# First experts' row lists by matrix products, and the slot table written in two passes of the expert loop

## The chip, the cores and the metric

One core of one Trainium2 chip runs the whole program as a single launch. The metric is the device time of that launch in microseconds. Before the change it is 1580.52 us, the median of three runs (1579.43 to 1581.09).

## What is computed

A residual block over 512 tokens and 16 meta tokens, width 1024: an input projection, a convolution branch and an mLSTM branch, an output projection, and then the part that this change touches, a mixture of 32 experts of which each token takes its best four.

```python
logits = xt @ router_w + router_b
top_val, top_idx = lax.top_k(logits, TOP_K)          # 4 of 32
gates = jax.nn.softmax(top_val, axis=-1)
...
hcat = xb @ w1[e] + b1[e]                            # 1024 x 2048
act = h_glu * sigmoid(1.702 * h_glu) * (h_lin + 1)   # both clamped at 7
ys = act @ w2[e] + b2[e]                             # 1024 x 1024
...
out = rms_norm(h + sum of gates * ys of each token's four experts)
```

## The kernel before, in words

The first third of the program (up to about 530 us) is the projections and the two branches. Then the router scores are made, and the expert loop runs: for expert 0 to 31 one pass, each with up to 96 tokens ("slots"). A pass multiplies the expert's tokens, transposed in `xT`, by the first weight matrix (192 records of L1613), DVE and ACT make the activation (L2096 to L2109), and a second product (192 records of L1642) makes the results, which DVE copies to `y_out` in three strips with the bias (L2127). The weights come through a ring of 12 buffers of 1 MB, one whole expert; SP asks for the next expert's piece as soon as TensorE has released a buffer (`ring_used`). A pass therefore needs two things: its weights, and its tokens.

The tokens come by row gathers that POOL issues one pass ahead. For pass n+1 POOL copies that expert's list into `piece_now` (L712) and issues three indirect DMAs from the row store `u_rows` into `xs` (L706, each after a small paced step, L705, that waits for a ring buffer). DVE transposes `xs` into `xT` (L2118) when all three have landed. Before POOL may gather, it must have sent the results of the pass before: three indirect DMAs of `y_out` into `y_rows` by `row_now` (L779, each after a step on `carrier`, L697), and it waits for their landing. So in steady state POOL does, in every pass: copy `row_now` (L769), three results out, wait for landing, copy `piece_now`, three gathers.

The lists come from a table in HBM, `slot_table`. For each of the 16 columns of token choices (4 tiles of 128 tokens times 4 choices) one indirect DMA of 128 four-byte entries writes the token's code to the place (slot, expert) (L730, `places_out`). After all 16 have landed, 16 loads bring the table back as `code_of` (L749), and 15 POOL operations (L755 to L759) turn it into `piece_of` (which rows to gather) and `row_of` (where results go) for all experts.

Two experts don't wait for the table. Expert 0's tokens are picked by TensorE directly: DVE makes a 0/1 matrix `in_slot` of tokens by slots (L1997), and TensorE multiplies the token rows by it (L1556); DVE transposes the product into `xT` (L2039). Expert 1's gather list is a product too: `in_second`, a 0/1 matrix for expert 1, times the token numbers (L1601), scaled by DVE into `piece_now` (L2048, 12 small operations). From expert 2 on, and for all result rows (expert 0's too), the table is needed.

The order on POOL around the change is written out by hand: eight scatters of the table as soon as the first two tiles' places are known, the three gathers for expert 1, eight more scatters paced by `ring_used` and `hid_mm` during pass 0, then the 16 loads, the arithmetic, a load of `last_g`, and the loop over the passes.

Of the kernel before, what the change touches and what calls it, by code (L numbers as in the profile page):

```python
# [78 lines left out]
PASSES = -(-SEQ // SLOTS)  # L79
SPREAD = 8  # L80
TURNS = 32 // SPREAD
NONE = 1 << 14
# [28 lines left out]
def hybrid_block(nc, x, meta_tokens, norm_mix_g, w_in, b_in, conv_dw_w, conv_dw_b, conv_ln_g, conv_ln_b,  # L111
# [3 lines left out]
    with ctx:  # L115
        def sem(name):
            return ctx.enter_context(nc.semaphore(name))
# [157 lines left out]
        in_second = at("in_second", [P, TT, SLOTS], F32, ffn_at[0] + size([P, (TT + 1) * SLOTS]) + size([P, P], BF16))  # L275
        token_no = at("token_no", [P, TT], F32, ffn_at[0] + size([P, (2 * TT + 1) * SLOTS]) + size([P, P], BF16))
        assert size([P, (2 * TT + 1) * SLOTS]) + size([P, P], BF16) + size([P, TT]) <= size([P, TG, 2 * GRP])
        hid = in_stage("hid", [P, TG, 2 * GRP])
# [90 lines left out]
        u2_mm, u2T_made, logits_mm, place_mm = sem("u2_mm"), sem("u2T_made"), sem("logits_mm"), sem("place_mm")  # L369
        moe_consts, mask_made, dest_made, table_set, table_written = sem("moe_consts"), sem("mask_made"), sem("dest_made"), sem("table_set"), sem("table_written")  # L370
        tables_made, passes_made, shifted, gate_exp = sem("tables_made"), sem("passes_made"), sem("shifted"), sem("gate_exp")
# [207 lines left out]
        def _(pool):  # L579
# [93 lines left out]
            nc.gpsimd.iota(code, [[TOPK * P, TT], [1, TOPK]], base=0, channel_multiplier=TOPK)  # L673
            nc.gpsimd.iota(token_no, [[P, TT]], base=0, channel_multiplier=1, allow_small_or_imprecise_dtypes=True)
# [3 lines left out]
            nc.gpsimd.iota(slot_no, [[32, TG], [1, SPREAD], [SPREAD, TURNS]], base=0, channel_multiplier=0, allow_small_or_imprecise_dtypes=True)  # L678
            chain(nc.gpsimd.memset(earlier, 1.0))
# [19 lines left out]
            def request_rows(turn=None):  # L699
# [10 lines left out]
            def gather(n, copied, turn=None):  # L710
# [3 lines left out]
                request_rows(turn)  # L714

# [3 lines left out]

            def places_out(i):  # L720

                pool.wait_ge(dest_made, i + 1)
                for m in range(TOPK * i, TOPK * (i + 1)):
                    if i >= 2:
                        late = m - 2 * TOPK
                        if late < KT - LATE:
                            pool.wait_ge(ring_used[late], 1)
                        else:
                            pool.wait_ge(hid_mm, late - (KT - LATE) + 1)
                    pool.indirect_dma_start(out=table, out_offset=bass.IndirectOffsetOnAxis(ap=dest[:, m:m + 1], axis=0),  # L730
                                            in_=code[:, m:m + 1], in_offset=None).then_inc(table_written, 16)
# [8 lines left out]
            pool.sem_inc(idx_step, 1)  # L740
# [5 lines left out]
            by_turn = table.rearrange("(x b a e) o -> b a x (e o)", b=TURNS, a=SPREAD, e=NE)  # L746
# [3 lines left out]
            pool.wait_ge(rows_in, 16 * CG * TURNS)  # L750
            for t in range(TG):
# [8 lines left out]
            pool.dma_start(last_g, final_norm_g.rearrange("(a d) -> a d", a=1).to_broadcast([P, D])).then_inc(last_g_in, 16)  # L760
            pool.wait_ge(y_emptied, 16 * KT)
            pool.wait_ge(passes_made, 1)
            passes = pool.value_load(n_passes[0:1, 0:1], min_val=1, max_val=PASSES)
            with pool.Fori(0, passes) as q:
# [7 lines left out]
                with pool.Fori(0, NE - 1) as e:  # L772
                    n = rows_of_expert(e)
                    pool.wait_ge(idx_step, n * IDX + 3 + TG)
                    for t in range(TG):

                        pool.wait_ge(y_made, n * TG + (t + 2))
                        carry_wait(1 + t)
                        pool.indirect_dma_start(out=y_dram, out_offset=bass.IndirectOffsetOnAxis(ap=row_now[:, t:t + 1], axis=0),  # L779
                                                in_=y_out[:, t], in_offset=None, bounds_check=last_row,  # L780
                                                oob_is_err=False).then_inc(y_stored, 16)

                    pool.wait_ge(y_stored, (q * (NE - 1) + e + 1) * (16 * TG))
                    carry_wait(1 + TG)
                    pool.wait_ge(xT_made, (n + 2) * TG)
                    gather(n + 2, n * IDX + 8 + TG, n + 2)

                n = rows_of_expert(NE - 1)
# [355 lines left out]
        def _(pe):  # L1144
# [455 lines left out]
            for i in range(TT):  # L1600
                last = nc.tensor.matmul(banks[0:SLOTS, SECOND_BANK, 0:1], in_second[:, i], token_no[:, i:i + 1], start=i == 0, stop=i == TT - 1)  # L1601
            last.then_inc(place_mm, 1)

            pe.wait_ge(passes_made, 1)
# [88 lines left out]
        def _(dve):  # L1693
            steps = [0]

            def chain(ins):

                steps[0] += 1
                ins.then_inc(dve_step, 1)
                dve.wait_ge(dve_step, steps[0])  # L1700
# [343 lines left out]

            dve.wait_ge(place_mm, TT + 2)
            for g in range(CG):
                for t in range(TG):
                    nc.vector.tensor_scalar(piece_now[32 * g:32 * (g + 1), t:t + 1], banks[32 * t:32 * (t + 1), SECOND_BANK, 0:1],  # L2048
                                            float(CG), float(g), ALU.mult, ALU.add).then_inc(tables_made, 1)
            dve.wait_ge(gate_exp, 1)  # L2050
# [174 lines left out]
```

## Time and profile before

| | |
|---|---|
| median of 3 runs | 1580.52 us |
| the profiled execution's own time | 1593.28 us |
| its span (first to last instruction) | 1591.5 us |
| mean granted TensorE clock | 0.987 of full |
| TensorE busy | 1537.9 us (97%) |
| DVE, POOL, ACT busy | 744.5, 533.4, 282.6 us |
| mean HBM and DMA traffic | 309 GB/s |

Times in the views are microseconds from the start of the span. "Idle before, releaser" says how long an engine did nothing before an instruction, and what ended it. The chain of waits follows the work that ended last back from the end; an entry "DMA a<-b" in it is the time from the issue of a transfer to its landing, and "issue" time in which nothing that the profile shows was waited for. TensorE's records are modelled at their ends, so back-to-back records mean that TensorE was fed, not that it was at its peak. The profiled execution is 12.8 us longer than the median of the runs.

### The profile page before, as it was taken

Reading aid. Unit: us, or ns where it says so; the run is one execution under the profiler, and the core shown is the slowest. Engines: PE = TensorE matmul, PEld = TensorE weight load, DVE = VectorE, ACT = ScalarE, POOL = GpSimd, SP = SyncE. Lnnn points to the kernel's source line nnn. Section 1 sums busy time; section 2 is a strip of 40 time slices with the busy share of each in tenths; the row PEclk is TensorE's granted clock in tenths of the full one; section 3 lists DMA queues with packets and bytes.
Section 4 is the critical chain, followed back from the end, with each engine's and each line's share of the span. In section 5 each row is a group of like instructions: output and inputs, shape, how many; then the busy total and the mean of one; then the engine's idle time right before and its main releaser. Section 6 shows DMA issues by size and latency. Waiting matters only on the chain.

```text
span 1591.5 us, 38141 instructions
## 1 busy us (share of the span) xinstructions
PE 1537.9 (97%) x15984; PEld 857.2 (54%) x15984; DVE 744.5 (47%) x1563; ACT 282.6 (18%) x406; POOL 533.4 (34%) x689
## 2 busy tenths in 40 slices
PE   7999999999999796999999999999999999999996
PEld 6998988877889532334333333433333343333334
DVE  4799898015242633344335334433533443353367
ACT  5333134346221300001001000100100010010001
POOL 7334333462343445222221222222122222212225
PEclk9999999999999898999999999999999999999998
DMA  7553243221276298999999999999999999999996
GB/s 218 159 181 111 78 144 98 84 75 53 80 291 229 67 334 348 362 417 420 419 418 418 420 418 418 420 418 418 418 419 418 416 421 419 418 419 420 418 418 248
DMA packets 132020, 492.27 MB, mean 309 GB/s; under 512 B 16301, under 2 KB 74085, under 8 KB 82308
## 3 DMA queue, kind: packets, MB, share of 16 engines
q1 hardware_dynamic: 111892, 463.30, 73.3%
q0 software_dynamic: 10448, 17.26, 3.0%
q10 hardware_dynamic: 9632, 11.03, 2.2%
q8 instruction: 35, 0.57, 0.2%
q14 instruction: 13, 0.11, 0.0%
HBM read 475.46 MB, written 24.87 MB: 314 GB/s over the span
## 4 chain that ended last, share of the span: by engine, by line
PE 89%; POOL 3%; DVE 2%; DMA 2%; issue 1%; ACT 1%; SPq 1%; another core or an unknown queue 1%; POOLq 0%; DVEq 0%; ACTq 0%
PE banks L1613 40%; PE banks L1150 28%; PE banks L1642 19%; DMA stage<-in_w_in_dram 1%; POOL code_of L749 1%; DMA code_of<-slot_table 1%; SPq L464 0%; DMA slot_table<-code,dest 0%; DMA xs<-u_rows,piece_now 0%; PE banks L1509 0%; PE banks L1382 0%; POOL h_res L804 0%; DVE h_res L2174 0%; POOL w_lo L629 0%
## 5 line engine op out<-in xcount | busy, mean ns | idle before, releaser
L1613 PE MATMUL banks<-w_ring,xT 128*32 128x512 f32 x6144 | 668.9, 595 | 20.7 <-DVE xT L2118 14.9
L1613 PEld LDWEIGHTS banks<-w_ring,xT 128*32 128x32 f32 x6144 | 190.2, 110 | 479.8 <-issue 474.2
L1642 PE MATMUL banks<-w_ring,actT 128*32 128x256 f32 x6144 | 338.1, 379 | 0.2
L2096 DVE TENSOR_TENSOR hid<-banks,bias_now 128x512 f32<-128x512 f32 x96 | 63.9, 665 | 470.7 <-PE banks L1613 470.7
L1642 PEld LDWEIGHTS banks<-w_ring,actT 128*32 128x32 f32 x6144 | 189.9, 110 | 156.3 <-issue 20.9
L638 POOL TENSOR_TENSOR w_lo<-stage,w_hi 128x2048 fp32r<-128x2048 f32 x38 | 175.3, 4613 | 258.0 <-ACT w_hi L857 258.0
L697 POOL TENSOR_TENSOR carrier<-carrier 1x1 f32<-1x1 f32 x161 | 32.2, 200 | 578.3 <-DVE y_out L2127 418.1
L1124 ACT ACTIVATE sig<-hid 128x256 f32<-128x256 f32 x96 | 40.0, 417 | 918.8 <-DVE hid L2097 900.8
L1150 PE MATMUL banks<-u_hi,w_hi 128*128 128x264 f32 (+1 forms) x528 | 176.5, 334 | 1.0 <-POOL w_lo L629 1.0
L1150 PE MATMUL banks<-u_hi,w_lo 128*128 128x264 f32 (+1 forms) x528 | 175.0, 331 | 0.0
L1150 PE MATMUL banks<-u_lo,w_hi 128*128 128x264 f32 (+1 forms) x528 | 174.6, 331 | 0.0
L1778 DVE SCALAR_TENSOR_TENSOR banks<-conv_in,taps,banks 128x512 f32<-128x512 f32 x224 | 151.1, 750 | 0.1
L706 POOL DMA_INDIRECT xs<-u_rows,piece_now x99 | 103.4, 1045 | 20.5 <-issue 16.8
L1150 PEld LDWEIGHTS banks<-u_hi,w_hi 128*128 128x128 f32 x528 | 99.6, 189 | 11.3 <-POOL w_lo L629 1.3
L1150 PEld LDWEIGHTS banks<-u_lo,w_hi 128*128 128x128 f32 x528 | 99.5, 188 | 10.1
L1150 PEld LDWEIGHTS banks<-u_hi,w_lo 128*128 128x128 f32 x528 | 99.5, 188 | 9.5 <-issue 0.2
L779 POOL DMA_INDIRECT y_rows<-y_out,row_now x93 | 94.6, 1018 | 15.4 <-issue 15.4
L857 ACT ACTIVATE w_hi<-stage 128x2048 fp32r<-128x2048 f32 x40 | 76.4, 1910 | 105.1 <-PE banks L1150 99.0
L2127 DVE TENSOR_TENSOR y_out<-banks,bias_now 128x256 f32<-128x256 f32 x96 | 40.7, 424 | 101.1 <-PE banks L1642 96.8
L2106 DVE TENSOR_TENSOR act_v<-hid,sig 128x256 f32<-128x256 f32 x96 | 59.7, 622 | 3.3
L705 POOL TENSOR_TENSOR pace<-carrier 1x1 f32<-1x1 f32 x99 | 19.3, 195 | 83.9 <-PE banks L1613 83.1
L2109 DVE STREAM_TRANSPOSE actT<-act_v 128x256 f32<-128x256 f32 x96 | 42.8, 446 | 3.3
(306 smaller groups left out, 1483.1 us busy)
## 6 DMA issues: line engine op xcount, KB each, us to landing
w_ring<-in_expert_w_dram SPq DMA_DIRECT2D x384, 1024.0 KB
stage<-in_w_in_dram SPq DMA_DIRECT2D x20, 1024.0 KB, 5.2
stage<-in_w_in_dram SPq DMA_DIRECT2D x16, 512.0 KB, 5.7
y_rows<-empty_row ACTq DMA_DIRECT2D x8, 1024.0 KB, 4.9
y_in<-y_rows SPq DMA_DIRECT2D x4, 2048.0 KB, 22.2
stage<-in_conv_pw_w_dram SPq DMA_DIRECT2D x4, 1024.0 KB, 5.2
stage<-in_mlstm_out_w_dram SPq DMA_DIRECT2D x4, 1024.0 KB, 5.2
stage<-in_w_out_dram SPq DMA_DIRECT2D x4, 1024.0 KB, 5.3
```

The lines of the kernel that those rows point to most:

```text
L638: nc.gpsimd.tensor_tensor(w_lo[:, s], stage[:, s], w_hi[:, s].bitcast(F32), ALU.subtract).then_inc(w_lo_made[s], 1)
L706: pool.indirect_dma_start(out=xs[:, t], out_offset=None, in_=u2_pieces, in_offset=bass.IndirectOffsetOnAxis(ap=piece_now[:, t:t + 1], axis=0),
L779: pool.indirect_dma_start(out=y_dram, out_offset=bass.IndirectOffsetOnAxis(ap=row_now[:, t:t + 1], axis=0), in_=y_out[:, t], in_offset=Non ...
L857: nc.scalar.activation(w_hi[:, s], stage[:, s], ACT.Copy).then_inc(w_hi_made[s], 1)
L1150: last = nc.tensor.matmul(dst, l, r, start=(k == 0 and n == 0), stop=(k == KT - 1 and n == 2))
L1613: last = nc.tensor.matmul(banks[32 * g:32 * (g + 1), t].rearrange("p (c j) -> p c j", j=64), xT[:, t, k], units, start=k == 0, stop=k == K ...
L1642: last = nc.tensor.matmul(banks[32 * g:32 * (g + 1), 3 + t, 0:GRP], actT[:, t, k], w2_ring[k // 2][:, k % 2, GRP * g:GRP * (g + 1)], start ...
L1778: nc.vector.scalar_tensor_tensor(out=to, in0=src, scalar=taps[:, ct, w:w + 1], in1=acc, op0=ALU.mult, op1=ALU.add).then_inc(conv_step, 1)
L2096: own(nc.vector.tensor_tensor(hid[:, t], banks[:, t], bias1, ALU.add))
L2106: own(nc.vector.tensor_tensor(act_v[:, t].rearrange("p (c q j) -> p c j q", q=2, j=32), lin.rearrange("p (c j q) -> p c j q", q=2, j=32), ...
L2109: nc.vector.transpose(actT[:, t].rearrange("p k s -> p (k s)"), act_v[:, t]).then_inc(actT_made, 1)
L2127: nc.vector.tensor_tensor(y_out[:, t], banks[:, 3 + t, 0:GRP], bias2, ALU.add).then_inc(y_made, 1)
```

## The change

It makes four edits.

1. Expert 2's gather list and expert 0's result list come from TensorE products as well. DVE makes a third selection matrix `in_third` (4 operations) and, for the code of each token's choice of expert 0, `first_codes` and `first_code` (2 operations), all ahead of the transposes that TensorE waits for. TensorE does 4 more products with `in_third` and 4 with `in_slot` and `first_code`. DVE writes the results with 24 small operations in place of 12, into columns 1 and 2 of `piece_of` and column 0 of `row_of`.
2. All 16 scatters move behind the row requests: 2, 3 and 4 of them behind the three gathers for expert 1 (pass 0), and 2, 2 and 3 behind the three gathers for expert 2 (pass 1). From the third on, a scatter waits until the one two before it has landed.
3. POOL's work of pass 0 (results of expert 0, gathers for expert 2) is written out ahead of the table; the loop starts at expert 1.
4. The table comes back by 4 loads of 32 partitions in place of 16 loads of 8; the slots are numbered plainly.

```diff
-            pool.wait_ge(table_set, 16)
-            for i in range(2):
-                places_out(i)
...
-            request_rows()
-            for i in range(2, TT):
-                places_out(i)
-            pool.wait_ge(table_written, 16 * TT * TOPK)
+            gather(1, 1, 1, (range(0, 2), range(2, 5), range(5, 9)))
+            pool.wait_ge(tables_made, 2 * CG * TG)
+            nc.gpsimd.tensor_copy(row_now, row_of[:, :, 0]).then_inc(idx_step, 1)
+            pool.wait_ge(idx_step, 3 + TG)
+            pool.wait_ge(y_emptied, 16 * KT)
+            results_out(0, 1)
+            pool.wait_ge(xT_made, 2 * TG)
+            gather(2, 8 + TG, 2, (range(9, 11), range(11, 13), range(13, 16)))
+            for half in table_written:
+                pool.wait_ge(half, 16 * (TT * TOPK // 2))
             for g in range(CG):
-                for b in range(TURNS):
-                    pool.dma_start(code_of[32 * g + b:32 * (g + 1):TURNS], by_turn[b]).then_inc(rows_in, 16)
+                pool.dma_start(code_of[32 * g:32 * (g + 1)], table.rearrange("(x j e) o -> j x (e o)", j=32, e=NE)).then_inc(rows_in, 16)
...
+            def places_out(columns):
+                for m in columns:
+                    pool.wait_ge(dest_made, m // TOPK + 1)
+                    if m > 1:
+                        pool.wait_ge(table_written[m % 2], 16 * (m // 2))
+                    pool.indirect_dma_start(out=table, ..., in_=code[:, m:m + 1], in_offset=None).then_inc(table_written[m % 2], 16)
...
+            for i in range(TT):
+                last = nc.tensor.matmul(banks[0:SLOTS, SECOND_BANK, 1:2], in_third[:, i], token_no[:, i:i + 1], ...)
+            for i in range(TT):
+                last = nc.tensor.matmul(banks[0:SLOTS, SECOND_BANK, 2:3], in_slot[:, i], first_code[:, i:i + 1], ...)
...
+            for i in range(TT):
+                slots_of(in_third, i, 2).then_inc(in_slot_made, 1)
+            chain(nc.vector.scalar_tensor_tensor(out=first_codes, in0=expert_f, scalar=0.0, in1=code_no, op0=ALU.is_equal, op1=ALU.mult))
+            nc.vector.tensor_reduce(first_code, first_codes, axis=AX.X, op=ALU.add).then_inc(in_slot_made, 1)
             for t in range(TG):
                 dve.wait_ge(rows_mm, TG if t else 1)
                 nc.vector.transpose(xT[:, t].rearrange("p k s -> p (k s)"), first_xs(t)).then_inc(xT_made, 1)
```

On POOL, from the first row request on, the order before (`moe_consts` and the like in brackets are the semaphores waited for):

```order
L697 TENSOR_TENSOR carrier<-carrier 1x1 [waits u2_stored3,tables_made,u2_stored2,u2_stored0,u2_stored1]
L705 TENSOR_TENSOR pace<-carrier 1x1
L706 DMA xs<-u_rows,piece_now 128x256
L705 TENSOR_TENSOR pace<-carrier 1x1
L706 DMA xs<-u_rows,piece_now 128x256
L705 TENSOR_TENSOR pace<-carrier 1x1
L706 DMA xs<-u_rows,piece_now 128x256
L730 DMA slot_table<-code,dest 18432x1 [waits ring_used0,dest_made]
L730 DMA slot_table<-code,dest 18432x1 [waits ring_used1]
```

The same engine with the change, from the results of expert 0 to the table loads:

```order
L741 DMA y_rows<-y_out,row_now 8192x256
L701 TENSOR_TENSOR carrier<-carrier 1x1 [waits y_stored]
L718 COPY piece_now<-piece_of 128x3 [waits xT_made]
L701 TENSOR_TENSOR carrier<-carrier 1x1 [waits idx_step]
L709 TENSOR_TENSOR pace<-carrier 1x1 [waits ring_used0]
L710 DMA xs<-u_rows,piece_now 128x256
L732 DMA slot_table<-code,dest 18432x1 [waits table_written1,dest_made]
L732 DMA slot_table<-code,dest 18432x1 [waits table_written0,dest_made]
L709 TENSOR_TENSOR pace<-carrier 1x1 [waits ring_used2]
L710 DMA xs<-u_rows,piece_now 128x256
L732 DMA slot_table<-code,dest 18432x1 [waits table_written1,dest_made]
L732 DMA slot_table<-code,dest 18432x1 [waits table_written0,dest_made]
```

Before, no scatter waits for another, and the last is issued in pass 0. Now the last seven stand behind the landing of expert 0's results, and each waits for a landing.

On DVE, around the transposes of expert 0's tokens, before:

```order
L1997 SCALAR_TENSOR_TENSOR in_second<-slot_no,banks,mask 128x96 x4
L2039 STREAM_TRANSPOSE xT<-banks 128x256 [waits rows_mm] x3
L2008 TENSOR_TENSOR picked<-one_hot,banks 128x128
L2010 TENSOR_REDUCE place<-picked 128x4 [waits dve_step]
L2011 SCALAR_TENSOR_TENSOR dest<-place,expert_f 128x4 [waits dve_step]
```

and with the change:

```order
L2012 SCALAR_TENSOR_TENSOR in_second<-slot_no,banks,mask 128x96 x4
L2012 SCALAR_TENSOR_TENSOR in_third<-slot_no,banks,mask 128x96 x4
L2054 SCALAR_TENSOR_TENSOR first_codes<-expert_f,code_no 128x16
L2055 TENSOR_REDUCE first_code<-first_codes 128x4 [waits dve_step]
L2058 STREAM_TRANSPOSE xT<-banks 128x256 [waits rows_mm] x3
```

Six operations now stand between `in_second` and the transposes that start expert 0.

## Rows read from the trace of the kernel before

**Rows 1.** The page, chain that ended last: shares of the span by engine, by line.

```profile
PE 89%; POOL 3%; DVE 2%; DMA 2%; issue 1%; ACT 1%; SPq 1%; another core or an unknown queue 1%; POOLq 0%; DVEq 0%; ACTq 0%
```

**Rows 2.** Busy time by stretch: passes 0 and 1, the gap, passes 2 and 3.

```profile
core 0: us, PE busy (x) PEld busy (x) DVE busy (x) ACT busy (x) POOL busy (x), PEclk, DMA share, GB/s
550.67:584.14 33.47, 33.47 (x384) 12.27 (x388) 18.74 (x66) 4.03 (x6) 15.11 (x21) 0.92 0.77 270
584.14:616.33 32.19, 32.03 (x388) 11.85 (x380) 9.21 (x19) 2.53 (x4) 19.08 (x34) 1.00 1.01 387
616.33:631.18 14.85, 0.00 (x1) 0.01 (x1) 1.24 (x5) 0.00 (x0) 4.35 (x10) 0.64 0.90 368
631.18:663.83 32.65, 32.65 (x388) 12.28 (x392) 14.62 (x37) 2.53 (x4) 10.35 (x20) 0.95 0.74 284
663.83:694.79 30.96, 30.96 (x388) 11.84 (x384) 12.07 (x30) 2.54 (x4) 7.95 (x16) 1.00 1.02 420
```

**Rows 3.** Waits of TensorE, 545 to 680 us: us in total, times, longest.

```profile
PE banks L1613 <- DVE xT L2118: 14.9, 1, 14.9
PE banks L1613 <- DVE xT L2039: 5.8, 1, 5.8
```

**Rows 4.** The chain in order of time, 574 to 684 us: start, us, what.

```profile
574.27 6.06 DMA slot_table<-code,dest
580.33 0.29 issue
580.62 9.08 POOL code_of L749 x15
589.70 8.72 DMA code_of<-slot_table
...
598.51 0.36 POOL token_part L755
...
609.83 0.16 POOL row_now L769
...
624.12 5.80 DMA xs<-u_rows,piece_now
...
631.18 22.29 PE banks L1613 x192
653.47 10.36 PE banks L1642 x192
663.83 20.60 PE banks L1613 x192
```

**Rows 5.** POOL in order of time, a steady pass: start, us, operation, idle before.

```profile
695.38 0.18 POOL L697 TENSOR_TENSOR carrier<-carrier 1x1 f32<-1x1 f32 x1 [2.10 <-DVE y_out L2127]
695.72 0.98 POOL L779 DMA_INDIRECT y_rows<-y_out,row_now  x1 [0.16 <-issue]
701.52 0.18 POOL L697 TENSOR_TENSOR carrier<-carrier 1x1 f32<-1x1 f32 x1 [4.82 <-DMA y_rows<-y_out,row_now]
...
702.54 1.06 POOL L706 DMA_INDIRECT xs<-u_rows,piece_now  x1 [0.26 <-issue]
```

**Rows 6.** POOL in order of time, a scatter in pass 0.

```profile
562.77 0.96 POOL L730 DMA_INDIRECT slot_table<-code,dest  x1 [1.19 <-PE banks L1613]
```

**Rows 7.** DVE in order of time, 542 to 585 us.

```profile
542.91 1.02 DVE L1997 SCALAR_TENSOR_TENSOR in_second<-slot_no,banks,mask 128x96 f32<-128x96 f32 x4
543.84 0.45 DVE L2039 STREAM_TRANSPOSE xT<-banks 128x256 f32<-128x256 f32 x1
549.75 0.78 DVE L2039 STREAM_TRANSPOSE xT<-banks 128x256 f32<-128x256 f32 x2 [5.46 <-remote]
...
554.76 0.18 DVE L2056 SCALAR_TENSOR_TENSOR gate_pick<-expert_f,gate_w 128x16 f32<-128x16 f32 x1
554.97 0.17 DVE L2057 TENSOR_REDUCE gate_last<-gate_pick 128x4 f32<-128x16 f32 x1
...
584.39 0.42 DVE L2127 TENSOR_TENSOR y_out<-banks,bias_now 128x256 f32<-128x256 f32 x1 [2.36 <-PE banks L1642]
```

**Rows 8.** TensorE in order of time: the products for expert 1's list.

```profile
543.98 0.84 PE L1601 MATMUL banks<-token_no,in_second 128*96 128x1 f32 x8 [0.91 <-issue]
```

**Rows 9.** The table's loads (L749): DMA to landing us, min, median, max.

```profile
DMA to landing us min/median/max: 2.8/6.9/8.7
```

**Rows 10.** DMA issues of the whole run: KB each, median us to landing.

```profile
slot_table<-no_code SPq DMA_DIRECT2D x1, 72.0 KB, 1.9
```

More of the change, by code:

```diff
@@ L275, in hybrid_block @@
         in_second = at("in_second", [P, TT, SLOTS], F32, ffn_at[0] + size([P, (TT + 1) * SLOTS]) + size([P, P], BF16))
-        token_no = at("token_no", [P, TT], F32, ffn_at[0] + size([P, (2 * TT + 1) * SLOTS]) + size([P, P], BF16))
-        assert size([P, (2 * TT + 1) * SLOTS]) + size([P, P], BF16) + size([P, TT]) <= size([P, TG, 2 * GRP])
+        lists_at = ffn_at[0] + size([P, (2 * TT + 1) * SLOTS]) + size([P, P], BF16)
+        token_no = at("token_no", [P, TT], F32, lists_at)
+        first_code = at("first_code", [P, TT], F32, lists_at + size([P, TT]))
+        code_no = at("code_no", [P, TT, TOPK], F32, lists_at + 2 * size([P, TT]))
+        first_codes = at("first_codes", [P, TT, TOPK], F32, lists_at + 2 * size([P, TT]) + size([P, TT * TOPK]))
+        in_third = at("in_third", [P, TT, SLOTS], F32, lists_at + 2 * size([P, TT]) + 2 * size([P, TT * TOPK]))
+        assert size([P, (3 * TT + 1) * SLOTS]) + size([P, P], BF16) + 2 * size([P, TT]) + 2 * size([P, TT * TOPK]) <= size([P, TG, 2 * GRP])
         hid = in_stage("hid", [P, TG, 2 * GRP])
@@ L673, in _ @@
             nc.gpsimd.iota(code, [[TOPK * P, TT], [1, TOPK]], base=0, channel_multiplier=TOPK)
-            nc.gpsimd.iota(token_no, [[P, TT]], base=0, channel_multiplier=1, allow_small_or_imprecise_dtypes=True)
+            nc.gpsimd.iota(token_no, [[P, TT]], base=-NONE, channel_multiplier=1, allow_small_or_imprecise_dtypes=True)
+            nc.gpsimd.iota(code_no, [[TOPK * P, TT], [1, TOPK]], base=-NONE, channel_multiplier=TOPK, allow_small_or_imprecise_dtypes=True)
             nc.gpsimd.iota(expert_id, [[1, NE]], base=0, channel_multiplier=0, allow_small_or_imprecise_dtypes=True)
@@ L677, in _ @@
             nc.gpsimd.memset(zeros, 0.0)
-            nc.gpsimd.iota(slot_no, [[32, TG], [1, SPREAD], [SPREAD, TURNS]], base=0, channel_multiplier=0, allow_small_or_imprecise_dtypes=True)
+            nc.gpsimd.iota(slot_no, [[1, SLOTS]], base=0, channel_multiplier=0, allow_small_or_imprecise_dtypes=True)
             chain(nc.gpsimd.memset(earlier, 1.0))
@@ L697, in carry_wait, with request_rows @@
                 nc.gpsimd.tensor_tensor(carrier[:, 1 + i:2 + i], carrier[:, 0:1], carrier[:, 0:1], ALU.add).then_inc(idx_step, 1)
-            def request_rows(turn=None):
+            def request_rows(turn=None, between=None):
                 carry_wait(0)
@@ L708, in request_rows, with gather @@
                                             bounds_check=last_piece, oob_is_err=False).then_inc(xs_in, 16)
-            def gather(n, copied, turn=None):
+                    if between is not None:
+                        places_out(between[t])
+            def gather(n, copied, turn=None, between=None):
                 nc.gpsimd.tensor_copy(piece_now, piece_of[:, :, bass.ds(n, 1)].rearrange("p t o -> p (t o)")).then_inc(idx_step, 1)
                 pool.wait_ge(idx_step, copied)
-                request_rows(turn)
+                request_rows(turn, between)
             u2_pieces = u2_dram.rearrange("n (g c) -> (n g) c", g=CG)
@@ L718, in _, with results_out @@
             last_row = pool.to_reg(Y_ROWS - 1)
[L720 to L729, printed above, removed]
-                    pool.indirect_dma_start(out=table, out_offset=bass.IndirectOffsetOnAxis(ap=dest[:, m:m + 1], axis=0),
-                                            in_=code[:, m:m + 1], in_offset=None).then_inc(table_written, 16)
+            def places_out(columns):
[3 more added lines that the diff above has]
+                        pool.wait_ge(table_written[m % 2], 16 * (m // 2))
+                    pool.indirect_dma_start(out=table, out_offset=bass.IndirectOffsetOnAxis(ap=dest[:, m:m + 1], axis=0),
+                                            in_=code[:, m:m + 1], in_offset=None).then_inc(table_written[m % 2], 16)
+            def results_out(n, stored):
+                for t in range(TG):
+                    pool.wait_ge(y_made, n * TG + (t + 2))
+                    carry_wait(1 + t)
+                    pool.indirect_dma_start(out=y_dram, out_offset=bass.IndirectOffsetOnAxis(ap=row_now[:, t:t + 1], axis=0),
+                                            in_=y_out[:, t], in_offset=None, bounds_check=last_row,
+                                            oob_is_err=False).then_inc(y_stored, 16)
+                pool.wait_ge(y_stored, stored * (16 * TG))
+                carry_wait(1 + TG)
             pool.wait_ge(table_set, 16)
-            for i in range(2):
-                places_out(i)
             for i in range(TT):
@@ L739, in _ @@
             pool.wait_ge(tables_made, CG * TG)
[L740 to L746 removed]
+            gather(1, 1, 1, (range(0, 2), range(2, 5), range(5, 9)))
[8 more added lines that the diff above has]
+                pool.wait_ge(half, 16 * (TT * TOPK // 2))
             for g in range(CG):
[L748 to L750 removed]
+                pool.dma_start(code_of[32 * g:32 * (g + 1)], table.rearrange("(x j e) o -> j x (e o)", j=32, e=NE)).then_inc(rows_in, 16)
+            pool.wait_ge(rows_in, 16 * CG)
             for t in range(TG):
@@ L770, in rows_of_expert @@
                     return n
-                with pool.Fori(0, NE - 1) as e:
+                with pool.Fori(first_expert, NE - 1) as e:
                     n = rows_of_expert(e)
                     pool.wait_ge(idx_step, n * IDX + 3 + TG)
[L775 to L784, printed above, removed]
+                    results_out(n, q * (NE - 1) + e + 1)
                     pool.wait_ge(xT_made, (n + 2) * TG)
                     gather(n + 2, n * IDX + 8 + TG, n + 2)
+                pool.reg_mov(first_expert, 0)
                 n = rows_of_expert(NE - 1)
@@ L1602, in _ @@
             last.then_inc(place_mm, 1)
+            pe.wait_ge(in_slot_made, 3 * TT + 1)
+            for i in range(TT):
+                last = nc.tensor.matmul(banks[0:SLOTS, SECOND_BANK, 1:2], in_third[:, i], token_no[:, i:i + 1], start=i == 0, stop=i == TT - 1)
+            last.then_inc(place_mm, 1)
+            for i in range(TT):
+                last = nc.tensor.matmul(banks[0:SLOTS, SECOND_BANK, 2:3], in_slot[:, i], first_code[:, i:i + 1], start=i == 0, stop=i == TT - 1)
+            last.then_inc(place_mm, 1)
             pe.wait_ge(passes_made, 1)
@@ L2043, in _ @@
             nc.vector.tensor_tensor(gate_w, best[:, :, 0:TOPK], best[:, :, 0:1].to_broadcast([P, TT, TOPK]), ALU.subtract).then_inc(shifted, 1)
[L2045 to L2049, printed above, removed]
+            dve.wait_ge(place_mm, TT + 4)
+            for to, from_cols, at_col in ((piece_of, slice(0, 2), 1), (row_of, slice(2, 3), 0)):
+                for g in range(CG):
+                    for t in range(TG):
+                        nc.vector.tensor_scalar(to[32 * g:32 * (g + 1), t, at_col:at_col + from_cols.stop - from_cols.start],
+                                                banks[32 * t:32 * (t + 1), SECOND_BANK, from_cols],
+                                                float(CG), float(CG * NONE + g), ALU.mult, ALU.add).then_inc(tables_made, 1)
             dve.wait_ge(gate_exp, 1)
```

7 lines of the change are left out of this document (3 added, 4 removed).

## The prediction, made before the changed kernel was run

> **What bounds the kernel now.** I read the shares of the chain first: 89% of the span is TensorE [rows 1]. So a change elsewhere counts only where TensorE stands still. The stretches of the expert loop show where: a steady pass takes 30.96 us with TensorE full, pass 0 takes 33.47 because it begins at the low clock, and between pass 1 and pass 2 lie 14.85 us with no product at all [rows 2]. TensorE's own waits say what ended that gap: the transposes of the gathered rows for expert 2 [rows 3]. Pass 2 then begins at a lower granted clock, 0.95 on average, and its first product takes 22.29 us against 20.60 in pass 3 [rows 2, 4].
>
> The chain in order of time says why those rows were late [rows 4]. The last scatter of the table is issued at 574.27 and lands 6.06 later; 16 loads are issued from 580.62 on and the last lands at 598.42, 17.8 us in all; the arithmetic starts at 598.51; `row_now` for expert 0 is copied at 609.83; results go out and land, the gathers go out, the last one 5.80 before it lands, and TensorE starts at 631.18. From the start of the arithmetic to that start is 32.7 us, and nothing in it can be moved ahead of the table. The prize is 14.85 us plus the slow start of pass 2 (32.65 - 30.96 = 1.7), 16.5 us in all.
>
> **What the change does to that chain.** It takes expert 2 off the table, but expert 1's results and expert 3's rows still need it. So the question is whether the table is ready one pass later. Without any gap pass 3 would begin at 616.33 + 30.96 = 647.3.
>
> (1) Added ahead of expert 0. Six DVE operations stand before the transposes: four like `in_second` (1.02 for four) and two like the small pair at 554.76, whose starts lie 0.21 apart [rows 7]: 1.02 + 0.42, with a wait between them 1.5 us. TensorE's 16 added records cost at most twice the 0.84 of the eight that stand there [rows 8]; half of them can run while DVE still works and the rest under the transposes, so I take nothing for them. Below, the 1.5 could vanish: DVE stands 5.46 us before its second transpose for a reason that the profile doesn't name [rows 7], and the six could run in that time. Above, 1.5 + 1.7 = 3.2. I take 1.5, since a wait without a name may as well come after the new work as cover it. It delays everything behind it. DVE's 12 added list operations lie in pass 0 with DVE free, cost nothing there, and POOL doesn't read the second half of them before expert 0's results.
>
> (2) Pass 0 on POOL. The gathers for expert 1 now wait for ring buffers and have scatters between them. TensorE's third release let a scatter go at 562.77 [rows 6]; 1.5 later the second gather can go. Then scatter 2 goes at about 565.6, and 4, 6 and 8 each follow a landing. With 5 us per landing the last is issued at 580.6, before expert 0's third result strip (584.39 + 0.42 + 1.5 = 586.3 [rows 7]); with the 6.1 of a loaded pass at 583.9, which puts the results back by up to 1.8. DMA was less loaded in this pass (share 0.77 against 1.01 in the next [rows 2]), so I take 5 and no delay. The row gathers for expert 1 land by 579 and are not late.
>
> (3) Results of expert 0. From the strip's carrier step to the issue is 0.34, from the issue to the step behind the landing 5.80, and from there to the first gather's issue 1.02 [rows 5]. With a small step ahead: 586.3 + 0.1 + 0.34 + 5.8 + 1.0 = 593.6. The gather takes 1.06, and with 0.3 of issue scatter 9 goes at 595.0.
>
> (4) The hops. Scatter 11 waits for 9, 13 for 11, 15 for 13, and the loads for 15: four landings in a row, each under full weight traffic. A scatter has one landing row, 6.06 plus 0.29 to the next issue; results take 5.8 [rows 4, 5]. I take 6.1 for the first three and 6.35 for the last: 595.0 + 18.3 + 6.35 = 619.6 for the first load, against 580.62, 39.0 later. Bounds per hop: 1.9, a plain write of the same table with DMA free [rows 10], and 8.7, the slowest landing of a table load [rows 9]. Traffic in pass 1 is full, so the loaded rows are nearest. The gathers for expert 2 stand between these scatters; the last goes at about 603.8 and lands near 609.6, while TensorE needs them at 617.8, so they are covered by 8 us.
>
> (5) The loads. Before, 17.8 us for 16. Four need 3 x 0.6 for issue (9.08 for 15 [rows 4]) and then a landing between the median 6.9 and 8.7 [rows 9]: 8.7 to 10.5, I take 9.0. That gives back 8.8. Bounds: 1.8 + 2.8 = 4.6, and the old 17.8.
>
> (6) All the rest of the chain, arithmetic, results, gathers and transposes, is the same work in the same order: no change.
>
> **The sum.** 39.0 - 8.8 = 30.2 later, so TensorE starts pass 3 at 631.18 + 30.2 = 661.4, after a wait of 661.4 - (647.3 + 1.5) = 12.6 us. It starts at the low clock as pass 2 did, takes 32.65, and pass 4 begins at 694.05. Before it began at 694.79 [rows 2]. The gain is 0.7 us: the gap moves by one pass and stays nearly as long. Against the median of the runs that is 1579.8 us. The profiled execution is 12.8 us longer than that median; I carry over the difference only. About 0.2%, 3.2 us, is what a measurement of this kernel can tell from no change.
>
> **The rivals.**
>
> *Short hops (faster).* If a scatter, which carries only four bytes per row, lands in 4.5 us instead of 6.1, four hops give 6.4 us more, 0.7 + 6.4 = 7.1 gained: 1573.4. For it speaks the 1.9 of the idle write [rows 10], against it 6.06 for the very same transfer [rows 4] in a pass less loaded than the one it goes to. Chance 0.25.
>
> *The gap vanishes (much faster).* If scatters land in about 2 us they are bound by issue alone: eight issues of about 1.3 behind scatter 9 bring the last to 605.5 and the loads to 607.8, 11.8 earlier than in the sum, and the gap of 12.6 falls to 0.8; shorter landings of results and gathers take the rest. Pass 4 would then begin at 648.8 + 31.0 = 679.8, 15.0 earlier: 1565.5. Against it speak all loaded landings, 5.8 and above [rows 4, 5]. The Trainium skill ("DMA: Bandwidth & Descriptors", section "Anatomy of one DMA — SWDGE (gpsimd) path") gives a fixed cost of about 2.0 us per such transfer, most of it the write receipt, and by that this rival would be the likeliest; the trace here disagrees with 6.06. Chance 0.05.
>
> *The loads are not cheaper (slower).* The table is read in the same 2304 runs of 128 bytes (32 partitions by 18, four times; before 8 by 18, sixteen times). If the time goes with the runs under full weight traffic and not with the number of loads, the 17.8 us stay, the 8.8 are not given back, and pass 3 starts at 670.2: 0.7 - 8.8 = -8.1, 1588.6. It decides from a load time of 9.0 + 3.9 = 12.9 on. For it: the loads' landings grow from 2.8 to 8.7 over the sixteen [rows 9], as of something that queues up. Against it: that growth is only 5.9 us over 9.08 of issuing [rows 4], so most of the 17.8 is issue. The Trainium skill (same page, section "Why a DMA increments its semaphore by 16 and not by 1") says that one descriptor moves one contiguous run, so the number of descriptors stays; no row here counts them. Chance 0.21, half of it with part of the loss (14 us, 1584.8).
>
> *Late pass 0.* Both upper ends of (1) and (2), +1.7 and +1.8, make 2.8 us slower, 1583.3, still inside what counts as the same. Chance 0.05.
>
> **How the numbers follow.** My forecast, the moved gap with little gained, has 0.44; with late pass 0 that makes 0.49, of which 0.03 fall out on the slow side: same 0.46. Faster: 0.25 + 0.05 = 0.30. Slower: 0.21 + 0.03 = 0.24. The range goes down to hops of 4 us (4 x 2.1 + 0.7 = 9.1 gained, 1571.5) and up to loads of 15.7 us (0.7 - 6.7 = 6 lost, 1586.5). It leaves out the vanished gap, the full loss on the loads and a few of the short hops, under 2 in 10. The forecast's own range is 1577.3 to 1583.7.
>
> **What would show it.** No gap ahead of pass 2, and one of about 12.6 us ahead of pass 3, ended by the transposes of gathered rows, with the low clock behind it. On POOL: scatter 9 near 595, scatters 11, 13 and 15 about 6 us apart, the first load near 620, the arithmetic near 629. Pass 0 starting 1.5 later than 550.67. I am wrong if pass 3 follows pass 2 directly, if the scatters lie 4 us or less apart, if the four loads take over 13 us, or if a gap stands ahead of pass 2 as well.

## The result, and the profile after

The changed kernel takes 1587.74 us (median of 7 runs, 1586.30 to 1590.01) against 1581.09 us (1579.38 to 1583.03) of the kernel before: ratio 1.0043, 95% interval 1.0031 to 1.0054, 6.65 us slower. The forecast was 1579.8 us and the range ended at 1586.5.

The gap did move by one pass, as forecast. TensorE's waits after, answering to [rows 3]:

```profile
PE banks L1628 <- DVE xT L2139: 19.6, 1, 19.6
```

It is ended by the transposes of expert 3's rows, and it is longer than the 14.85 us it replaces. Busy time by pass, passes 0 to 2, the gap and pass 3, answering to [rows 2]:

```profile
core 0: us, PE busy (x) PEld busy (x) DVE busy (x) ACT busy (x) POOL busy (x), PEclk, DMA share, GB/s
543.42:574.40 30.98, 30.98 (x385) 12.98 (x388) 19.04 (x74) 4.03 (x6) 12.34 (x16) 1.00 0.83 286
574.40:605.56 31.16, 31.15 (x389) 12.84 (x381) 10.68 (x27) 2.53 (x4) 14.87 (x23) 1.00 1.01 402
605.56:636.52 30.96, 30.96 (x384) 12.84 (x384) 11.01 (x26) 2.53 (x4) 11.60 (x20) 1.00 1.02 394
636.52:656.35 19.83, 0.21 (x5) 0.01 (x1) 1.24 (x5) 0.00 (x0) 8.88 (x18) 0.61 0.79 318
656.35:689.83 33.48, 33.48 (x385) 12.31 (x388) 14.62 (x37) 2.53 (x4) 10.38 (x20) 0.92 0.73 275
```

Pass 2 now follows pass 1 directly, and pass 3 restarts at a lower granted clock, 0.92, in 33.48 us instead of 30.96. The chain in order of time, answering to [rows 4], shows what the gap was waiting for:

```profile
548.99 6.93 DMA slot_table<-code,dest
556.66 5.98 DMA slot_table<-code,dest
563.38 6.72 DMA slot_table<-code,dest
570.85 4.78 DMA slot_table<-code,dest
...
580.68 6.25 DMA y_rows<-y_out,row_now
...
589.24 5.73 DMA slot_table<-code,dest
595.72 6.59 DMA slot_table<-code,dest
603.05 5.68 DMA slot_table<-code,dest
609.48 5.76 DMA slot_table<-code,dest
...
615.87 2.10 POOL code_of L764 x3
617.97 9.09 DMA code_of<-slot_table
627.15 0.36 POOL token_part L770
...
652.35 2.74 DMA xs<-u_rows,piece_now
...
656.35 23.30 PE banks L1628 x192
```

Eight scatter landings in a row, four in pass 0 and four in pass 1, lie on the path, with expert 0's results between them. Before, only the last scatter's landing was on it. POOL in order of time shows the place where the two halves meet:

```profile
576.38 0.97 POOL L732 DMA_INDIRECT slot_table<-code,dest  x1 [2.36 <-DVE y_out L2148]
...
577.97 1.01 POOL L741 DMA_INDIRECT y_rows<-y_out,row_now  x1 [0.16 <-issue]
579.34 1.01 POOL L741 DMA_INDIRECT y_rows<-y_out,row_now  x1 [0.16 <-issue]
580.68 1.00 POOL L741 DMA_INDIRECT y_rows<-y_out,row_now  x1 [0.16 <-issue]
```

The ninth scatter leaves at 576.38. The view names `y_out` as its releaser, but its code waits only for a landing, the one of the chain's 570.85 + 4.78 = 575.63. The three results then go out without a wait between them, because all three strips had been made: in the run without these waits (e2) they leave at 570.27, 572.10 and 575.55, as they are made.

### The profile page after: what moved, and what is told of

The parts are those of the page before. It is cut to its first block, busy times and chain, and to the rows that moved or that the text cites. A ratio compares the mean times of both kernels' runs of the same rounds, so it can differ in the third digit from the quotient of the medians.

```text
span 1588.3 us, 38303 instructions
## 1 busy us (share of the span) xinstructions
PE 1536.9 (97%) x16000; PEld 864.2 (54%) x16000; DVE 746.7 (47%) x1581; ACT 282.7 (18%) x406; POOL 528.0 (33%) x679
## 4 chain that ended last, share of the span: by engine, by line
PE 64%; issue 18%; POOL 7%; DMA 6%; DVE 2%; ACT 1%; SPq 1%; POOLq 1%; DVEq 0%; ACTq 0%
PE banks L1158 28%; PE banks L1628 23%; PE banks L1657 11%; DMA slot_table<-code,dest 3%; POOL y_rows L741 2%; POOL xs L710 2%; DMA y_in<-y_rows 1%; DMA y_rows<-y_out,row_now 1%; DMA stage<-in_w_in_dram 1%; POOL carrier L701 1%; DMA code_of<-slot_table 1%; SPq L467 0%; PE banks L1517 0%; POOL h_res L812 0%; PE banks L1390 0%
## 5 line engine op out<-in xcount | busy, mean ns | idle before, releaser
L1628 PE MATMUL banks<-w_ring,xT 128*32 128x512 f32 x6144 | 667.8, 594 | 19.7 <-DVE xT L2139 19.6
L1657 PEld LDWEIGHTS banks<-w_ring,actT 128*32 128x32 f32 x6144 | 192.7, 110 | 153.7 <-issue 19.3
L710 POOL DMA_INDIRECT xs<-u_rows,piece_now x99 | 105.3, 1064 | 19.5 <-issue 15.9
L2139 DVE STREAM_TRANSPOSE xT<-xs 128x256 f32<-128x256 f32 x96 | 33.9, 404 | 34.7 <-DMA xs<-u_rows,piece_now 34.7
```

Source lines behind the costliest of these rows:

```text
L1628: last = nc.tensor.matmul(banks[32 * g:32 * (g + 1), t].rearrange("p (c j) -> p c j", j=64), xT[:, t, k], units, start=k == 0, stop=k == K ...
L1657: last = nc.tensor.matmul(banks[32 * g:32 * (g + 1), 3 + t, 0:GRP], actT[:, t, k], w2_ring[k // 2][:, k % 2, GRP * g:GRP * (g + 1)], start ...
```

## The experiments

**e1: the kernel before, once more.** In the profiled execution of before DVE stood 3.05 and 5.46 us for a reason that the profile did not name. No edit.

> The kernel before, unchanged, for a second profile. Theory A (the two waits of 3.1 and 5.5 us on DVE, of which the first profile does not name the releaser, belong to that one execution, as it took 1593 us where the runs take 1581): pass 0 begins near 542, takes 31.0 us in place of 33.5 because TensorE keeps its clock, and the gap ahead of pass 2 is about 16 us; time 1581. Theory B (they belong to every execution): pass 0 begins at 550.7, takes 33.5 us, and the gap is 14.9 us again.

1582.12 us, ratio 0.9998 (0.9989 to 1.0008). The waits without a name are gone, pass 0 starts at 539.99 and pass 1 ends at 601.93; the gap and the pass behind it:

```profile
601.93:619.22 17.29, 0.19 (x5) 0.01 (x1) 1.24 (x5) 0.00 (x0) 5.01 (x11) 0.64 0.87 355
619.22:652.41 33.19, 33.19 (x385) 12.32 (x389) 14.60 (x37) 2.53 (x4) 10.39 (x20) 0.93 0.73 278
```

The gap to compare with is 17.1 to 17.3 us, not 14.85: the prediction was built on an execution that had spent part of it earlier. So the change made the gap 2.5 us longer.

**e2: no scatter waits for another.**

```diff
-                    if m > 1:
-                        pool.wait_ge(table_written[m % 2], 16 * (m // 2))
```

> The changed kernel without the wait of a scatter for the landing of the one two before it (the loads still wait for all sixteen). Theory A (the landings in a row make the table late): expert 0's three results go out about 5 us earlier, scatters 9 to 15 are bound by their issue, about 1.3 us each, the first load is issued about 15 us earlier, and the gap of 19.6 us ahead of pass 3 falls to about 4.5 us; time about 1572.5 us. Theory B (the software queue serves a scatter only every 3 us or so, whoever waits): the last scatter lands as late as before, the gap stays at 15 us or more; 1584 to 1588 us.

1579.44 us, ratio to before 0.998 (0.9971 to 0.9989). The gap falls to 10.4 us. The waits are the loss, and without them the change gains 2.6 us; but they give 9.2 us of gap, not 15, so theory A has the cause right and the size too large.

**e3: sixteen loads of 8 partitions, as before, in the changed kernel.**

```diff
-                pool.dma_start(code_of[32 * g:32 * (g + 1)], ...)
+                for b in range(TURNS):
+                    pool.dma_start(code_of[32 * g + b:32 * (g + 1):TURNS], by_turn[b])
```

> The changed kernel with the table read by sixteen loads of 8 partitions and the slots numbered as before. Theory A (the time goes with the number of loads): 17.8 us from the first issue to the last landing in place of 11.3, the gap ahead of pass 3 grows by 6.5 us to about 26 us; time 1594 us. Theory B (it goes with the runs of 128 bytes, which are the same): 11 to 12 us, gap and time as with the change, 1587.7 us.

1590.82 us, ratio 1.0053 (1.0038 to 1.0068). POOL, from the first load to the arithmetic:

```profile
611.14 9.70 POOL L768 DMA_DIRECT2D code_of<-slot_table  x16 [5.25 <-DMA slot_table<-code,dest]
628.55 0.35 POOL L774 TENSOR_SCALAR token_part<-code_of 128x192 f32<-128x192 int32 x1 [7.70 <-DMA code_of<-slot_table]
```

17.4 us against 627.15 - 615.87 = 11.3 for four, both reading the same runs of 128 bytes. The rival that the loads are not cheaper is out; its point of decision was 12.9. Theory A's gap and time were too large: the gap is 21.7 us, not 26, since in this execution the first load goes 70.6 us behind the start of pass 0 (in e5 72.8) and the way from the arithmetic to TensorE takes 28.4 us (in e5 30.0).

**e4: the kernel before with the six DVE operations and eight products added, their results unused.**

> The kernel before with the six added operations of DVE and the eight added products of TensorE ahead of expert 0, whose results nobody reads; the order on POOL as before. Theory A: pass 0 begins 1.5 us later and everything behind it too, 1582.6 us. Theory B (covered by DVE's wait ahead of its second transpose): 1581.1 us. Theory C (TensorE's products add to it): 3.2 us, 1584.3 us.

1584.74 us, ratio 1.0017 (1.0008 to 1.0027): about 2.7 us over before. From the start of `in_second` to pass 0 it takes 3.83 us where e1 took 2.59, so the work itself costs 1.2, near theory A. The time is nearest to theory C, but not for its reason. In the profile a lower clock makes pass 0 1.7 us longer, and most of that is hidden again: the gap ahead of pass 2 is 15.5 us instead of 17.1. Its pass 6 starts 2.0 us later than that of e1 (747.29 against 745.29); of these 1.2 are the work, and most of the rest lies ahead of it. Busy time around pass 0's start (542.16), with the granted clock in the column PEclk:

```profile
540.00:542.00 2.00, 1.61 (x19) 1.53 (x18) 1.93 (x9) 0.00 (x0) 1.44 (x2) 1.00 0.02 1
542.00:544.00 2.00, 1.99 (x18) 0.71 (x21) 1.74 (x12) 0.22 (x1) 1.43 (x2) 0.87 0.01 0
544.00:546.00 2.00, 2.00 (x12) 0.46 (x8) 1.67 (x11) 1.28 (x1) 0.37 (x2) 0.50 0.01 0
546.00:548.00 2.00, 2.00 (x20) 0.65 (x16) 1.91 (x9) 0.00 (x0) 1.63 (x3) 0.78 0.31 41
```

For some 3 us TensorE gets half its clock (1.2 instead of 2.4 GHz), and pass 0's first product takes 22.50 us instead of 20.81.

**e5: the changed kernel once more; e6: its waits in pass 0 taken out.**

```diff
-                    if m > 1:
+                    if m > 8:
```

> The changed kernel, unchanged, for a second profile beside the next three. Theory A: the gap ahead of pass 3 is 18 to 21 us and ahead of pass 2 there is none; expert 0's third result goes out 4 to 5 us after DVE has made it; time 6 to 7 us over the kernel before.

> The changed kernel with the waits between scatters 0 to 8 (pass 0) taken away; those of scatters 9 to 15 (pass 1) stay. Theory A (both halves delay the table): expert 0's third result goes out as soon as it is made, 4 to 5 us earlier, all behind it too; the gap ahead of pass 3 falls to about 15 us, time 4 to 5 us under the changed kernel. Theory B (pass 0 covers its waits, as I had predicted): the gap and the time stay as with the change.

1588.60 us (ratio 1.0035, 1.0023 to 1.0047) and 1588.44 us (1.0032, 1.0019 to 1.0045): no difference, as theory B had it. But not for theory B's reason. In e5 expert 0's third result goes out 2.7 us after DVE has made it (578.28 against 575.56), less than the 4 to 5 expected; gap and time are as expected. In e6 the results do leave as they are made and the list arithmetic starts at 621.23 instead of 626.32 in e5. The gap shrinks only from 19.3 to 18.7, since the last gather, 2.74 us in the changed kernel's chain above, takes 6.42 here. DMA while it is under way, first e6, then the changed kernel, each with the stretch before:

```profile
642.00:647.10 5.10, 0.00 (x0) 0.00 (x0) 0.00 (x0) 0.00 (x0) 3.17 (x8) 0.50 1.01 421
647.10:653.52 6.42, 0.00 (x0) 0.00 (x0) 0.00 (x0) 0.00 (x0) 1.22 (x2) 0.50 0.90 360
```

```profile
646.00:650.00 4.00, 0.00 (x0) 0.00 (x0) 0.00 (x0) 0.00 (x0) 1.19 (x5) 0.50 1.03 422
650.00:652.35 2.35, 0.00 (x0) 0.00 (x0) 0.00 (x0) 0.00 (x0) 1.99 (x4) 0.50 0.53 195
652.35:655.09 2.74, 0.00 (x0) 0.00 (x0) 0.00 (x0) 0.00 (x0) 1.22 (x2) 0.50 0.25 75
```

With TensorE standing, the weight transfers go on until the ring is full. A gather issued after that lands in 2.7 us; one issued 5 us earlier runs beside the weights and lands at nearly the same moment. So lists that come 4.2 us sooner, counted from the end of pass 2 (e6 against e5), shorten the gap by 0.6.

**e7: all sixteen scatters unpaired and out by the end of pass 0; e8: the loads there too, ahead of expert 0's results.**

```diff
+            places_out(range(0, 8))
-            gather(1, 1, 1, (range(0, 2), range(2, 5), range(5, 9)))
+            gather(1, 1, 1, (range(8, 10), range(10, 13), range(13, 16)))
...
-            gather(2, 8 + TG, 2, (range(9, 11), range(11, 13), range(13, 16)))
+            gather(2, 8 + TG, 2)
```

> The changed kernel with no wait between scatters, the first eight issued ahead of expert 1's gathers while POOL is idle, as in the kernel before, the other eight behind those gathers in pass 0, none in pass 1; the loads follow expert 2's gathers. Theory A (only the place of the table in the chain made the loss): first load near 589, lists ready near 610, no gap ahead of pass 2 nor of pass 3; with 1.2 us for the products ahead of expert 0 and 1.7 for a cold first product, about 16 us under the kernel before, 1566 us. Theory B (rows that come by the same queue, or weights, are then late): a gap of 3 us or more ahead of pass 1, 2 or 3; 1570 us or more.

> As the run before, with the four loads issued at the end of pass 0, ahead of expert 0's results. Theory A (no gap is left to close): the time of the run before within 1 us, lists ready some 12 us earlier than there. Theory B (the run before still waits for the table): faster than it by its gap.

1573.71 us (0.9946, 0.9932 to 0.9960) and 1572.07 us (0.9939, 0.9925 to 0.9952): both beat both kernels. Neither has a gap, and passes 1 to 16 follow each other every 30.96 us. Theory A of e7 had the gaps right and the time 8 us too low; theory B had the time, but there is no gap ahead of pass 1, 2 or 3. e8's lists are ready 9 us earlier than e7's (598.7 against 607.7), its time is 1.6 us lower, and the two intervals overlap: no gap was left to close.

Both also put the first eight scatters back ahead of pass 0, where the kernel before has them and where DMA falls idle. In e8 each landing can be read. The three scatters issued from 540.00 to 542.54, with a DMA share of 0.02 and less, land in 2.1 to 2.9 us; the eight of pass 0, beside the weights and issued no closer together, in 4.2 to 6.2:

```profile
DMA to landing us min/median/max: 2.1/2.3/2.9
DMA to landing us min/median/max: 4.2/5.0/6.2
```

So the same form of transfer lands slowly where other traffic runs beside it, and the change moved its first eight scatters from ahead of pass 0 into that traffic.

Yet e7's pass 6 starts 17.4 us before that of e1 (727.86 against 745.29), and the median gains only half of that. TensorE and DMA in the long middle, e7 and then e1:

```profile
700.00:1100.00 400.00, 399.92 (x4972) 167.34 (x4968) 156.69 (x390) 32.92 (x52) 102.38 (x206) 1.00 1.02 419
1100.00:1500.00 400.00, 397.55 (x4836) 164.61 (x4832) 151.55 (x377) 31.51 (x51) 101.10 (x204) 1.00 1.02 419
```

```profile
700.00:1100.00 400.00, 400.00 (x4972) 153.18 (x4968) 156.07 (x389) 32.93 (x52) 102.98 (x207) 1.00 1.02 419
1100.00:1500.00 400.00, 400.00 (x4976) 153.26 (x4972) 156.89 (x390) 32.93 (x52) 102.74 (x207) 1.00 1.02 419
```

The weights run at 419 GB/s without a break in both. In e7 TensorE catches up with them and waits for the ring (time in total, times, longest):

```profile
PE banks L1656 <- DMA w_ring<-in_expert_w_dram: 1.8, 7, 0.4
PE banks L1627 <- DMA w_ring<-in_expert_w_dram: 0.8, 4, 0.2
```

From pass 6 to pass 31, 25 passes, e7 takes 1509.36 - 727.86 = 781.5 us where TensorE alone would take 25 x 30.96 = 774.0. So 7.5 us of what the closed gap gave is lost, to the weights as it seems. Only 2.6 us of it show as waits; in the rest the records, whose ends are modelled, stand back to back. Shown so far is the coincidence; e10 and e11 test it.

**e9: the changed kernel without the waits of pass 1** (`if 1 < m < 9:`); **e10 and e11: e7 with the list arithmetic done two and three times** (`for again in range(2):`, `range(3)` around L769 to L773), so that a gap comes back.

> The changed kernel with the seven waits of the scatters of pass 1 taken out, those of pass 0 kept. Theory A (both halves of the chain of landings cost): expert 0's results leave POOL some 5 us after they are made, as in the changed kernel (577.97 to 580.68 there); the seven scatters of pass 1 follow each other at the pace of their issue, the last at about 600 instead of 609.48, the loads at about 607.5 instead of 615.87. Of these 8.4 us the gap ahead of pass 3 gives back about 4 to 5, since the run without the waits of pass 0 had its lists 5 us earlier and its gap only 0.6 us shorter: gap 14 to 15, 1583 to 1585 us. Theory B (the waits of pass 1 make all of the difference, those of pass 0 none): the gap falls to the 10.4 of the kernel without any such wait, and the time to about 1579.5 us.

> The kernel with all sixteen scatters in pass 0 (1573.71 us, no gap ahead of any pass) with the arithmetic on the two lists done twice, 9.4 us more on POOL: the last gather for pass 3 is issued at about 633.4 instead of 623.95, and TensorE stands 3 to 6 us ahead of pass 3 and restarts at the lower clock, another 2 us. Theory A (the weight transfers set the end: they run without a break at 418 GB/s, and TensorE, 30.96 us for a pass in the early ones, waits for them in the later ones, 7.5 us in sum): the standing costs nothing in the end, the time is 1573 to 1575.5 us and the last pass starts at 1509 to 1511. Theory B (TensorE sets the end): 1579 to 1582 us.

> As the run before with the arithmetic done three times, 18.8 us more on POOL: a gap of 12 to 16 us ahead of pass 3 and 2 us of lower clock behind it. Theory A (the weight transfers set the end as long as TensorE loses less than 7.5 us): of the 14 to 18 us lost the first 7.5 cost nothing, and the time rises by 7 to 11 us over the 1573.71 us of the kernel with the arithmetic done once, to 1581 to 1585 us. Theory B (TensorE sets the end): by 14 to 18 us, to 1588 to 1592 us.

e9: 1581.30 us (0.9997, 0.9987 to 1.0007), gap 14.4: the gap is theory A's, the time lies between the two theories, 1.7 us below A's range and 1.8 above B's figure. TensorE's waits of e10 and of e11:

```profile
PE banks L1628 <- DVE xT L2139: 5.0, 1, 5.0
```

```profile
PE banks L1628 <- DVE xT L2139: 14.7, 1, 14.7
```

e10 takes 1574.33 us (0.9954, 0.9941 to 0.9968), 0.6 over e7 with a gap of 5.0 us; e11 takes 1584.21 us (1.0017, 1.0008 to 1.0026), 10.5 over e7 with one of 14.7. The runs of before beside these two were 1.25 us faster than those beside e7; with each median taken against its own, it is 1.9 and 11.8 us. Both times are inside theory A's ranges and outside theory B's; e10's last pass starts at 1511.63, 0.6 behind its range. e10 and e11, taken together, are 9.9 us apart for 9.7 us of gap. So the weight transfers set the end while TensorE loses less than about 7.5 us; beyond that the gap, and the slow restart behind it, count in full, within what these medians can tell.

## Why the prediction was wrong

The gap moved by one pass for the reason that the prediction gave. It failed on the length: 19.6 us instead of 12.6. Mis-sized were the delay of POOL in pass 0 (step 2), the hops (step 4) and the loads (step 5). Two costs had no term at all: the lower clock in pass 0, 1.7 us in some executions, and the waits for weights at the end, 1.4.

The steps of the sum can be set beside the runs, all counted from the first gather for expert 2 (us; the end of pass 2 is its start + 30.96):

| | forecast | after | e5 | e6, no waits in pass 0 | e9, none in pass 1 | e2, none |
|---|---|---|---|---|---|---|
| gather ahead of the end of pass 2 | 55.2 | 48.7 | 50.8 | 53.6 | 48.7 | 53.6 |
| (4) gather to first load | 26.0 | 28.0 | 29.0 | 27.8 | 18.7 | 20.1 |
| (5) loads to arithmetic | 9.0 | 11.3 | 11.3 | 11.1 | 11.5 | 11.3 |
| (6) arithmetic to TensorE | 32.7 | 29.2 | 30.0 | 33.6 | 33.1 | 32.8 |
| gap: the last three less the first | 12.5 | 19.8 | 19.5 | 18.9 | 14.5 | 10.6 |

**Step (2) failed first**, "5 us per landing ... so I take 5 and no delay". It read an average DMA share of 0.77 for pass 0 as a lighter load. The average hid an idle start: in the changed kernel pass 0 has 0.83, but that is 0.12 up to 548.00 and 0.89 to 1.04 from 549.00 on, where the scatters run. Their landings took 6.93, 5.98, 6.72 and 4.78, as long as those of pass 1. Expert 0's results left 5 us later than in e2 (in e5 2.7), beyond the upper bound of 1.8. The hops are one part of it: scatters 2 to 8 took (576.38 - 556.66) / 3 = 6.6 us for each landing, so the last went 33.0 us behind the start of pass 0, where the prediction had 28.4 (580.6 - 552.2) and at its bound 31.7. The base is the other part: its pass 0 lasted 33.47 us [rows 2], but here it lasted 30.98, and the third strip was ready 32.4 us behind the pass's start instead of 34.1.

**Step (4) and step (5) were too small** by 2.0 and 2.3 us. The hops are 6.4 to 7.3 us from issue to issue, not 6.1: a landing of 5.7 to 6.6, and 0.6 to 0.7 until the next scatter goes, of which only the last hop had an allowance. For the loads the landing was the slip: "between the median 6.9 and 8.7", taken at about 7.2, but the last of four wide ones took 9.09:

```profile
DMA to landing us min/median/max: 6.9/8.2/9.1
```

The median was of 16 loads a quarter as large [rows 9]. The saving was 18.2 (e1) - 11.3 = 6.9 us, by e3 17.4 - 11.3 = 6.1, instead of 8.8.

**Step (6), "no change", was off the other way** by 3.5 us: the last gather landed in 2.74 instead of 5.80 [rows 4], as the gap was long enough for the ring to fill. That hides an error when it is added up: with the waits of step (2) taken out (e6), step (6) is 33.6, and the gap 18.9 all the same. So the lateness of step (2) was the largest error in the account, but curing it alone is worth under 1 us. The curable cost is the chain of landings in pass 1: e9 takes 7.3 us less than e5, 6 us when each is taken against the runs of before beside it.

**The base was wrong by 2.2 us.** The gap of 14.85 belonged to an execution with 8.5 us of unexplained waits ahead of pass 0; in e1 it is 17.1. The end of the gap goes with the start of pass 0, 80.5 us behind it there, 79.2 in e1 and 79.4 in e4, so a slow pass 0 makes the gap shorter: it took 33.47, 30.98 and 32.67 us.

**Step (1) was about right** in the work, and had no term for the clock. DVE of the changed kernel in order of time, answering to [rows 7]:

```profile
540.54 1.02 DVE L2012 SCALAR_TENSOR_TENSOR in_third<-slot_no,banks,mask 128x96 f32<-128x96 f32 x4
541.48 0.16 DVE L2054 SCALAR_TENSOR_TENSOR first_codes<-expert_f,code_no 128x16 f32<-128x16 f32 x1
541.67 0.17 DVE L2055 TENSOR_REDUCE first_code<-first_codes 128x4 f32<-128x16 f32 x1
541.76 1.10 DVE L2058 STREAM_TRANSPOSE xT<-banks 128x256 f32<-128x256 f32 x3
```

541.76 - 540.54 = 1.2 us, against 1.5 forecast. TensorE's first record of pass 0 comes at 543.42, in e5 at 542.22, where e1 has 539.99; the rest of the difference lies ahead of the new operations and varies from run to run (by 1.2 us between two executions of the same kernel).

**Where the 6.65 us went**, by the pass starts of the profiled executions, e5 against e1: pass 0 starts 2.23 later; it takes 1.69 longer at the lower clock; from pass 2 to pass 3 it takes 50.45 us, where the pass with the gap took 48.25 (+2.20); the slow restart costs 33.91 instead of 33.19 (+0.72). That is 6.8 us at pass 6, and 1.4 more are lost in the last passes, where TensorE waits for weights: 8.3. These two executions lie 8.2 us apart, while the median of e5 is 6.1 over that of before; in the first profile of the changed kernel pass 0 kept its clock. So the parts show the kinds of loss, and not shares of the 6.65 to the tenth.

**The rivals.** Short hops: no hop of pass 1 in the chain above was under 6.3 us, from issue to issue. The vanished gap: its mechanism is not what happened, and e2, where the scatters of pass 1 are bound by issue, still has 10.4 us of gap. The fixed cost of about 2.0 us in the Trainium skill ("DMA: Bandwidth & Descriptors", section "Anatomy of one DMA — SWDGE (gpsimd) path") describes no landing here beside the weights (4.2 to 8.3 us for a scatter); near it are transfers with the weights not running, the scatters of e8 ahead of pass 0 (2.1 to 2.9) and the gathers behind the full ring (2.55 in e3, 2.74 in the changed kernel). That rival was also overpriced, as was "the prize ... 16.5 us in all": with no gap at all the time is 1572 to 1574 us, not 1565.5, since the weights become the bound. "Late pass 0" had the right place and only a third of the size in the results' delay, 1.8 against 5; but by e6 that delay costs next to nothing.

## What to carry to other kernels

A transfer that waits for the landing of the one before pays the full loaded latency each time, so such a pair wait costs far more than its issue: without the waits the change gains 2.6 us over before (e2) where with them it loses 6.65. With the scatters moved as well, eight back ahead of pass 0 and eight into pass 0, it gains 9 to 10 (e7, e8). Price a stall of the main engine against the slack of the stream that feeds it, not by its length: the first 5 us of gap cost 0.6 to 1.9, the next 10 cost 9.9. And before building on one execution, look for waits without a name in it, and read the load of a pass by the stretch in which the transfer runs, not by the pass's average.

## What the runs showed of the hardware

- With the weights at about 420 GB/s, an indirect scatter of 128 four-byte entries takes 4.2 (e8) to 8.3 us (e2, with several in flight) from issue to landing, the results 5.7 to 6.8, a row gather 5.8 to 6.4. With the weights not running it is 2.1 to 2.9 us for a scatter (e8, 540 to 545 us) and 2.55 (e3), 2.74 (changed kernel) and 3.14 (e5) for the row gather behind the full ring. Where in the transfer the added time is spent was not measured.
- Four table loads of 32 partitions take 11.0 to 11.5 us until the arithmetic starts, sixteen of 8 partitions 17.0 to 18.2, for the same bytes in the same runs.
- The granted clock fell to 0.50, the lower of its two levels, for some 3 us at pass 0's start in e2 to e6 and in e8, and stayed at 1.00 in the first profile of the changed kernel, e1, e7, e9, e10 and e11, where TensorE had done the same products ahead of it (e1: only eight of them). e5 and the first profile are the same program. What decides it stays open; it costs 1.7 us of TensorE's time each time, of which the gap hid most in e4 and the weights in e8.
